# Delta rule of a two-block model, from two chains of 256-token units to four chains of 128-token units

## The reference

```python
def step(s, inp):
    r_t, w_t, k_t, v_t, a_t, b_t = inp
    sa = jnp.einsum('bhvk,bhk->bhv', s, a_t)
    s = s * w_t[:, :, None, :] + sa[..., None] * b_t[:, :, None, :] + v_t[..., None] * k_t[:, :, None, :]
    y = jnp.einsum('bhvk,bhk->bhv', s, r_t) if emit else None
    return s, y
```

## Time and profile before

| | |
|---|---|
| median of 3 runs | 3953.07 us (3949.59 to 3955.18) |
| span of the profiled execution | 3941.6 us |
| time around the span, taken as median less span | 11.5 us |
| TensorE busy over the span | 3377.2 us, 86% |
| VectorE, ScalarE, GpSimd busy | 60%, 45%, 19% |
| mean granted TensorE clock | 0.933 |
| delta rule stage, first issue to the next stage's first issue | 771.7 to 1358.7 us |

### The profile page before, as it was taken

One profiled execution on the slowest core, in us unless ns is written; L12 is line 12 of the kernel. 1 busy time (PEld: TensorE's weight loads), 2 busy tenths in 40 slices (PEclk: granted clock), 3 DMA queues, 4 the chain that ended last, 5 costly groups with the idle time before them and its releaser, 6 DMA issues. The chain is left out here.

```text
span 3941.6 us, 97846 instructions
## 1 busy us (share of the span) xinstructions
PE 3377.2 (86%) x38463; PEld 2331.6 (59%) x38463; DVE 2360.6 (60%) x4245; ACT 1768.8 (45%) x2361; POOL 731.1 (19%) x706
## 2 busy tenths in 40 slices
PE   4999799677778587979998998999689999878789
PEld 0899788577677475733332333333267777666567
DVE  1688688655555466627776766776377574056631
ACT  0577577422222124307776766776222321156620
POOL 4000000043444200331221221222112333200000
PEclk7999899899899788989999999999899999988899
DMA  8354445421221255949889999953734323265452
GB/s 315 84 171 139 160 130 166 159 86 46 61 72 44 82 167 200 209 155 315 277 263 356 351 354 357 326 160 76 244 87 128 86 75 96 95 153 132 117 181 75
DMA packets 520291, 665.36 MB, mean 169 GB/s; under 512 B 77168, under 2 KB 423984, under 8 KB 516768
## 3 DMA queue, kind: packets, MB, share of 16 engines
q1 hardware_dynamic: 494576, 572.44, 45.2%
q0 software_dynamic: 25216, 86.62, 8.9%
q10 hardware_dynamic: 48, 0.05, 0.0%
HBM read 493.08 MB, written 165.94 MB: 167 GB/s over the span
## 5 line engine op out<-in xcount | busy, mean ns | idle before, releaser
L2600 PE MATMUL routed_p_gu<-routed_fixed,routed_x 128*32 128x512 f32 x3840 | 572.5, 600 | 0.0
L2600 PE MATMUL routed_p_gu<-moe_exp_w,routed_x 128*32 x1280 | 571.5, 600 | 0.7 <-DVE routed_fixed L2722 0.7
L2654 ACT COPY routed_fixed<-moe_exp_w 128x1024 f32 x320 | 332.6, 1047 | 222.1 <-DMA moe_exp_w<-in_exp_w_up_dram 86.3
L2722 DVE COPY routed_fixed<-moe_exp_w 128x1024 f32 x640 | 398.0, 681 | 51.3 <-DMA moe_exp_w<-in_exp_w_up_dram 42.9
L544 PE MATMUL front_ps<-front_a_high,front_w_high 128*128 128x320 f32 (+1 forms) x1120 | 362.7, 324 | 16.3 <-DVE front_w_low L797 13.4
L544 PE MATMUL front_ps<-front_a_low,front_w_high 128*128 128x320 f32 (+1 forms) x1120 | 353.8, 316 | 0.0
L544 PE MATMUL front_ps<-front_a_high,front_w_low 128*128 128x320 f32 (+1 forms) x1120 | 353.7, 316 | 0.0
L2600 PEld LDWEIGHTS routed_p_gu<-moe_exp_w,routed_x 128*32 128x32 f32 x1280 | 135.4, 111 | 356.2 <-issue 356.2
L3606 PE MATMUL pre_ps<-pre_a_high,pre_w_high 128*128 128x512 f32 x720 | 287.1, 399 | 13.3 <-ACT pre_xb L3753 6.7
L2615 PE MATMUL routed_p_y<-routed_wd,routed_hT 128*32 x640 | 290.4, 597 | 3.4 <-ACT routed_fixed L2665 3.4
L2615 PE MATMUL routed_p_y<-routed_fixed,routed_hT 128*32 128x512 f32 x1920 | 291.4, 597 | 0.0
(11 more groups left out here) (550 smaller groups left out, 7386.6 us busy)
## 6 DMA issues: line engine op xcount, KB each, us to landing
moe_exp_w<-in_exp_w_gate_dram SPq DMA_DIRECT2D x64, 1024.0 KB, 13.3
moe_exp_w<-in_exp_w_up_dram SPq DMA_DIRECT2D x64, 1024.0 KB, 16.4
routed_wd<-in_exp_w_down_dram SPq DMA_DIRECT2D x64, 1024.0 KB, 15.1
front_wt<-in_w_in_dram SPq DMA_DIRECT2D x70, 512.0 KB, 4.4
mod_w<-in_w_mod_dram SPq DMA_DIRECT2D x24, 1024.0 KB, 18.2
pre_wt<-in_w_in_dram SPq DMA_DIRECT2D x44, 512.0 KB, 4.0
out_a<-mix SPq DMA_DIRECT2D x24, 512.0 KB, 4.0
total<-out_none SPq DMA_DIRECT2D x24, 512.0 KB
```

Of the source, the lines that this page charges most:

```text
L2600: op = nc.tensor.matmul(p_gu[spot(s), :], x[:, b % 2, k, spot(s)], w, start=(k == 0), stop=(k == KD - 1))
L2654: nc.scalar.copy(fixed[:, place_of(b, c), 0, :], wgu[:, bass.ds(e % WS, 1), c * D:(c + 1) * D].rearrange("p o n -> p (o n)"))\
L2722: op = nc.vector.tensor_copy(fixed[:, place_of(b, c), s - 1, :], wgu[:, bass.ds(es[s] % WS, 1), c * D:(c + 1) * D].rearrange("p o n -> p ( ...
```

## The change

Only `rwkv_mix` and the layout of its DRAM inputs change. Four chains run, one for each group of 128 rows, `OFFSET` is 5. A unit is one tile of 128 tokens in each direction: 8 problems. Units 0 and 1 are context, 2 to 9 latent, and an eleventh round of slots holds only the last normalisation.

- turn: six turns of b, k and v. k and v are loaded with the two halves of their tokens exchanged, so that after the turn the b rows and k rows of one chunk lie on 128 rows together (`bk`); `uv` takes v beside what the inverse yields. ScalarE makes six copies of 64 x 256.
- prod: both products in one slot; VectorE masks in six instructions. zed moves into t0, ahead of the turns. GpSimd makes the first TT in four pieces of 64 x 128.
- t0 and, from level 2 on, each w slot turn the inverse by two full 128 x 128 turns; ScalarE copies TT, and VectorE's W waits for that copy. t makes T alone.
- The matrices m and n, query, wup and intra go. For each chunk: as (a times the state, plus zed), vn (the inverse times that), st (b and k stacked on 128 rows times u and v stacked, one product per state). GpSimd multiplies the state by its decay (`faded`) beside it.
- st1 of a latent unit makes the outputs: for each problem one product over 128 rows (`cc` with `uv`) and one over 64 rows (r with the state) into the same place.
- The normalisation follows each tile, spread over the slots of the next unit, 256 columns at a time. Bonus and gate are loaded and the results stored per tile.
- `tot` is loaded once for all; the loads of unit 0 of all four chains go first, then `tot` and lnx, and ScalarE, VectorE and GpSimd wait for these four.

```diff
-    OFFSET = 11
+    GROUPS = QT
+    OFFSET = 5
...
         def slots(n):
-            out = ["turn", "prodb", "prodk", "zed", "t0"]
+            norm = ["mean", "square", "var", "root", "norm", "back", "res", "gate"] if finishing(n) else []
+            if n == TILES:
+                return norm
+            out = ["turn", "prod", "t0"] + norm[0:1]
             for l in range(1, LEVELS + 1):
-                out += [f"w{l}", f"t{l}"]
...
+                out += [f"w{l}"] + norm[2 * l - 1:2 * l] + [f"t{l}"] + norm[2 * l:2 * l + 1]
+            return out + ["as0", "vn0", "st0", "as1", "vn1"] + (["st1"] if latent(n) or n < LAST else [])
...
+            for u in range(GROUPS):
+                load(0, u)
+            for d in range(2):
+                sp.dma_start(tot[:, :, d, :], rw["tot"][d].rearrange("(u p) c -> p u c", p=P)).then_inc(once, 16)
...
+                def turned_inverse():
+
+                    for e in range(2):
+                        op = nc.tensor.transpose(b[:, 0, span(TT_AT + e * P, P)], T[u][:, 2 * e:2 * e + 2, :], consts["ident"][:, :])
                     return op
...
                 elif p == "t0":
+                    DV.wait(pe, by_vector[u], n, "cc")
+                    for s, d, c, h in problems():
+                        nc.tensor.matmul(b[half(c), 1, span(2 * P + (2 * s + h) * HEAD, HEAD)], bkT[u][half(1 - c), 2 * d + h, :],
+                                         uv[u][half(1 - c), d, s, stacked(h)], start=True, stop=True)
                     PO.wait(pe, by_pool[u], n, "tt")
+                    for e in range(2):
+                        op = nc.tensor.transpose(b[:, 0, span(TT_AT + e * P, P)], TT[u][:, e], consts["ident"][:, :])
...
+                    if s == 1 and latent(n):
+                        for s, d, c, h in problems():
+                            y = b[half(c), h, span(Y_AT + (d if second(n) else 1 - d) * HEAD, HEAD)]
+                            nc.tensor.matmul(y, cc[u][:, c, h, d, :], uv[u][:, d, s, stacked(h)], start=True, stop=False)
+                            op = nc.tensor.matmul(y, x[half(h), R, d, half(c)], S[u][half(h), z, s, d, :], start=False, stop=True)
...
-                if p == "prodb":
+                if p == "prod":
                     DV.wait(pool, by_vector[u], n, "at")
-                    DV.wait(pool, by_vector[u], n - 1, f"tt{LEVELS}")
-                    PE.wait(pool, products[u], n - 1, "wup")
-                    first_level(slice(0, P), slice(0, P), slice(0, 2))
-                    for c in range(2):
-                        first_level(half(1 - c), half(c), slice(2, 4))
+                    PE.wait(pool, products[u], n - 1, f"t{LEVELS}")
+                    for h in range(2):
+                        for c in range(2):
+                            first_level(c, h)
                     pool.drain()
```

More of the change, by code:

```diff
@@ L1031, in slots @@
[L1031 to L1034, removed]
+                out += [f"w{l}"] + norm[2 * l - 1:2 * l] + [f"t{l}"] + norm[2 * l:2 * l + 1]
+            return out + ["as0", "vn0", "st0", "as1", "vn1"] + (["st1"] if latent(n) or n < LAST else [])
         def pe_steps(n):
-            out = ["ta", "tb", "tk", "tv", "prodb", "prodk", "zed", "t0"]
+            back = ["back"] if finishing(n) else []
@@ L1038, in pe_steps @@
+            if n == TILES:
+                return back
+            out = ["turn", "prod", "t0"]
             for l in range(1, LEVELS + 1):
[L1039 to L1042, removed]
+                out += [f"w{l}"] + (back if l == 3 else []) + [f"t{l}"]
@@ L1044, in dve_steps @@
+            return out + ["as0", "vn0", "st0", "as1", "vn1", "st1"]
         def dve_steps(n):
[L1045 removed]
+            norm = ["mean", "var", "norm"] if finishing(n) else []
+            if n == TILES:
+                return norm
+            out = ["at", "bk", "cc"] + norm[0:1]
             for l in range(1, LEVELS + 1):
[L1047 to L1049 removed]
@@ L1050, in dve_steps @@
[L1050 removed]
+                out += [f"w{l}"] + norm[l:l + 1]
+            return out + ["as0", "st0", "as1"] + (["st1"] if n < LAST else []) + (["y"] if latent(n) else [])
         def act_steps(n):
[L1053 to L1058 removed]
@@ L1060, in rwkv_mix @@
-        PE, DV, AC, PO = (Counts(UNITS, f) for f in (pe_steps, dve_steps, act_steps, pool_steps))
-        order = [(n, p) for n in range(UNITS) for p in slots(n)]
+            norm = ["square", "root", "res"] if finishing(n) else []
+            if n == TILES:
+                return norm
+            out = ["turn", "t0"]
+            for l in range(1, LEVELS + 1):
+                out += ([f"tt{l}"] if l > 1 else []) + (norm[l - 1:l] if l < 3 else []) + [f"t{l}"] + (norm[2:3] if l == 3 else [])
@@ new lines, in body @@
+                    if l > 1:
+                        AC.wait(pe, by_scalar[u], n, f"tt{l}")
+                    for e in range(2):
+                        for c in range(2):
+                            for h in range(2):
+                                old, step = TT[u][half(h), e, c, :], W[u][half(h), c, e, :]
+                                if l == LEVELS:
+                                    old, step = step, old
+                                op = nc.tensor.matmul(b[half(c), h, span(T_AT + e * HEAD, HEAD)], old, step, start=True, stop=True)
```

588 lines of the change are left out of this document (265 added, 323 removed).

## The result

The changed kernel takes 4190.86 us (median of 4 runs, 4186.76 to 4194.8) beside 3951.33 us for the kernel before in the same session: 1.0605 times as long, 95% interval 1.0588 to 1.0622, so 240 us slower. The forecast was slower, 4050 us with a range up to 4175: the sign is right, the size is less than half of it, and the result lies 16 us above the range.

What follows compares the result with a forecast made beforehand. No engine full: a hand-ordered chain of round trips bounds the stage. Slots 638 us against 555 (+83), start +13, end -12, queues and pauses +13: +97, 4039 of span, 4050 with 11.5 around it; range 3905 to 4175.

Steps and rivals of the forecast that it cites:

- The heavy round trips: Slots st1, turn and prod: never shared by two chains, so each paid 40 times; 13.3 us per latent unit.
- prod to the turn of TT: From prod through VectorE's masks and GpSimd's four pieces to t0: 5.2 us, 5.3 with the change of size.
- st1 to turn: State product, 16 output products, hand-overs and two state updates: 5.2 us in a latent unit, 1.2 without output.
- turn to prod: Six turns, six ScalarE copies of 256 columns and hand-overs: 2.7 to 2.8 us, kept as a wait.
- The alternating pair: Output products in st1: each neighbour has another array size, so 16 changes drain the array, 4.0 us.
- rival (a): Output products in st1: pair not drained, about 1.0 us, 97 us less in all, time 3953; chance 0.20.
- Start and end: Stage start 23.3 us against 10.2 (loads ahead of parameters, +13); end 10 instead of 22 (-12).
- The light steps: Two light steps between one unit's t0 and the next chain's st1: 3.0 us for both.
- the rule of the sum: In the hand-written order, a step lasts as long as its longest round trip, unless TensorE's own work is more.
- (d): The forecast itself: 4050 us, own range 4000 to 4110; chance 0.43.
- (c): TensorE's granted clock: waits behind prod drop it to 0.50 for half the time, 70 us more, 4120; chance 0.20.
- Rival (b): Whole stage: four chains cover each other, GpSimd sets the time, stage 450 instead of 587, 3815; chance 0.17.

Runs made afterwards that it cites:

- run 4: Changed kernel with GpSimd forming TT's first level in one product instead of four pieces, exchange of halves left out (other values); 4108.02 us, ratio 1.0398 to the kernel before.
- run 2: Changed kernel with the chains one slot apart instead of five (OFFSET 1), nothing else; 4042.66 us, ratio 1.0234 to the kernel before.
- run 1: Changed kernel with each unit's 16 output products grouped in fours by array size instead of alternating; 4059.33 us, ratio 1.0275 to the kernel before.
- run 5: Changed kernel with each unit's eight zed products computed three times into the same place, 640 products added; 4144.32 us, ratio 1.048 to the kernel before.
- run 6: Changed kernel with outputs grouped, T turned by 64x64 products, tot and parameter transfers ahead of the 40 loads, chains one slot apart; 3974.33 us, ratio 1.0062.
- run 8: Changed kernel with outputs grouped, tot and parameter transfers first, chains one slot apart, T still turned by full 128x128 turns; 3951.44 us, ratio 0.9992.
- run 11: Changed kernel with outputs grouped, parameters first, distance one, TT shared between GpSimd and VectorE, T turned by 64x64 products; 3965.56 us, ratio 1.0024.
- run 9: Changed kernel with outputs grouped, parameters first, distance one, full turns, VectorE forming two of TT's four pieces; 3939.72 us, ratio 0.9946, the fastest.

## Why the prediction was right in direction and short in size

**The heavy round trips: right.** prod to the turn of TT 5.5 us for 5.3, st1 to turn 5.45 (1134.12 to 1139.57) for 5.2, turn to prod 3.2 (1139.57 to 1142.78) for 2.8. The 0.4 is ScalarE's: its copies in a row start 0.377 us apart, 2.25 us for six (1140.48 + 1.50, 1141.99 + 0.74), where I had taken 0.10 less from the second on, 1.8. GpSimd's 128-wide operation, which no row showed, took 0.450 as estimated. The rows of both, ScalarE's as a timeline and GpSimd's as a group of instructions:

```profile
1140.48 1.50 ACT L1283 COPY rwmix_bk<-rwmix_ps 64x256 f32<-64x256 f32 x4 [0.40 <-PE rwmix_ps L1178]
1141.99 0.74 ACT L1283 COPY rwmix_uv<-rwmix_ps 64x256 f32<-64x256 f32 x2
...
L1408 POOL TENSOR_TENSOR rwmix_TT<-rwmix_at,rw_mask 64x128 f32<-64x128 f32 x160 | 72.0, 450 | 1013.2 <-DVE rwmix_at L1341 995.9 <-issue 0.4
```

Run 4 shows that the wait for GpSimd is paid in full, run 2 that it is the order that makes all of them be paid.

**The alternating pair: right.** 4.0 forecast, 4.1 measured; rival (a) falls with run 1. The Trainium skill (TensorEngine Tiling (Array Packing), Tiling Modes) says that changing the tiling mode drains the array. The trace agrees for an accumulating pair too, with 0.257 us from product to product.

**Start and end: right** (23.4 for 23.3, 11.4 for 10).

**The light steps: the term that was mis-sized.** Two light steps were put at 3.0 us; from the turn of TT to st1 a quarter at full clock takes 3.9:

```profile
1148.28 0.44 PE L1198 MATMUL rwmix_ps<-ident,rwmix_TT 128*128 128x128 f32 x2 [1.14 <-POOL rwmix_TT L1418]
...
1152.16 0.46 PE L1248 MATMUL rwmix_ps<-rwmix_uv,rwmix_bk 128*64 128x64 f32 x8
```

Part of it is a slip: TensorE's own work in the two steps was put at 2.0 and 1.4, the rule of the sum takes the larger of work and round trip, and that gives 3.4. The rest is that work and round trip aren't alternatives: slots of several chains stand one behind the other and a wait of 0.32 us falls in between (1150.77, for VectorE's W). With the 0.4 us of turn to prod and 0.2 to 0.25 each on the other two ways, a quarter at full clock is 18.05 for 16.3, and a round of four units some 5.4 us longer than forecast (its fourth quarter, four slots wide, is about right), some 43 us in the 8 latent rounds, and 12 in the two context ones (a quarter of 14.6 for 12.3).

**The clock: the step that failed.** Forecast (d) kept the clock of before and made the low clock a rival of its own, (c), at 0.20, with 70 us on top of (d): in the forecast's own sum the time at half clock stood at nothing. Rival (c)'s size was of the right order: 397 us at half clock, 362 of them in the middle, some 98 us. What was wrong was to call it a separate case. The waits behind prod that (d) rests on lower the clock (run 5), so whoever forecasts the waits has to put the clock into the same sum, and run 1 adds that the output burst, 4.1 us of sparse products, lowers it as well: 4050 + 98 = 4148, and with the light steps some 4190. The row that I set against it, a chain alone that kept 0.99 over 10.80 us with TensorE idle for nearly half of them, was a single one, at the stage's beginning, right after the clock had risen (0.50 from 755 to 784 us, where TensorE stood still up to 780); it says little on 40 such stretches in a row. The fall behind the 2.06 us pause, in the same rows, was the better guide. The Trainium skill (TensorE: Matmul & The Clock Gate, What's actually happening) says that the default state is throttled and activity releases it; the direction agrees with run 5, where more work meant 153 us less at half clock.

Adding up the middle: 138 us were missing. The slots took 55 more (light steps, turn to prod and the small rest); 13 had been added for queues and pauses, which don't show beside them; that leaves 42. The clock took some 98. Together 140, an estimate, with 0.27 as its softest number. The norm slots add nothing beyond this: the two norm rounds that can be read whole, from the first chain's prod to its next (1274.88, 1368.19, 1463.15), take 93.3 and 95.0 us for a forecast of 74, but 58 and 72 us of them are at half clock, which is 16 and 19 us; what is left, 78 and 76, is 2 to 4 over. One count of the prediction was wrong without consequence: SyncE's 240 loads before are 114 us of its queue at 0.475, not 240 us.

**Rival (b)**, four chains that cover each other, fell at the wait from prod to t0, the place named. But its idea wasn't empty: at distance one, with the outputs grouped, the start mended and TT shared, the stage runs in 574 us, under the 587 before, though far from the 450 of the rival. The distance alone gives 141 us of stage (run 2): it is the distance of five that takes this covering away.

**What should have shown it.** A stage of 685 us: no, 824. TensorE idle some 3 us ahead of the turn of TT: no, 1.15 there and 0.97 ahead of zed; the length of the way was right, but TensorE's own work, prod, zed and the others' slots, fills 3.4 of its 5.5 us. Output products near 4 us: yes. VectorE under 50%: yes, 32%. Granted clock under 0.8: yes, 0.76, the sign named for (c).

## What to carry to other kernels

In a hand-written order of several chains, count the steps that hold a heavy slot: at distance one the heavy slots of neighbouring chains overlap, at five they never do, and one constant was worth 148 us here. Products of different array sizes are issued in groups, since each alternation costs about 0.2 us. And waits or drawn-out products in TensorE's way can be priced twice, once as themselves and once through the clock; here the second price was half to two thirds of the first (run 1: 46 and 86 us, run 2: 57 and 91, run 4: 30 and 53).

## What the runs showed of the hardware that was not expected

**Work that pays by filling a wait.** 640 added products made the kernel 47 us faster (run 5), through the granted clock alone: a quarter at full clock stayed 18.05 us.

**The instruction supply of TensorE.** The pauses of run 6 come where short products at one array size follow each other without a wait. The DMA view of that run, from 1155 to 1175 us in 40 slices, shows when the queue of instructions (q8) moved. It is taken for TensorE's, because its blocks in the stage go with TensorE's records: 94 for 23808 (run 8), 111 for 28288 (run 6), 134 for 34176 (before).

```profile
GB/s 0 0 0 0 0 0 0 33 0 0 0 0 0 0 0 33 0 0 0 0 0 0 33 0 0 0 0 0 0 0 33 0 0 0 0 0 0 0 33 0
DMA packets 5, 0.08 MB, mean 4 GB/s; under 512 B 0, under 2 KB 0, under 8 KB 0
## 3 DMA queue, kind: packets, MB, share of 16 engines
q8 instruction: 5, 0.08, 1.8%
```

Blocks of 16 KB (0.08 MB in 5) arrive 3.5 to 4 us apart. Of the gaps of over 0.35 us for which the profile shows no releaser, between 780 and 1360 us, all 42 end 1.2 to 1.6 us after the last block has landed (worked out from the DMA records and the matmul rows; the pause above ends at 1165.02, the block before it landed at 1163.59), though only 9% of the time lies 1.2 to 1.7 us behind a block. The same holds for all 43 of run 11. The pauses are seen twice (runs 6 and 11, 45.5 and 51.3 us) and go with the full turns (runs 8 and 9, 2.1 and 3.6 us). The kernel before has 40 us of such pauses between 800 and 1340 us, the changed kernel none: they lie in the "10 us of queues and pauses" a round of the prediction, which also kept 1.3 us a round for them after the change. They carry the same mark: all 48 of over 0.35 us end 1.2 to 1.6 us behind a block. So the kernel before, too, seems to be held by its instructions for some 40 us; that the supply is the cause is inferred from this match and from runs 8 and 11, no view shows TensorE waiting for a block. The Trainium skill (Runtime: NRT & Kernel Launch, Instruction fetch mechanics) says that fetching is hidden because instructions are issued more slowly than they are filled in; the pauses of runs 6 and 11, each ending just behind a block, speak against it for products this short, and where they differ the measurement decides.
